# One decoder block on one core: 24 instead of 16 expert blocks loaded whole, and their schedule

## The reference, cut to what matters

```python
eid = take_along_axis(cand_i, pos)           # (token, head, 16)
gate = softmax(top_s)
act = gelu(einsum('bthkd,btd->bthk', peer_u[eid], h))
out = einsum('bthk,bthkd->btd', gate * act, peer_v[eid])
x = x + out
```

## Time and profile before

| what | value |
|---|---|
| runs shown | 2595.43, 2602.96, 2604.31 us, median 2602.96 |
| profiled execution, its own time | 2600.41 us |
| its span | 2598.8 us |
| PE, DVE, ACT, POOL busy in the span | 78%, 64%, 35%, 34% |
| moved by DMA | 746.40 MB, mean 287 GB/s |
| packets of the gathers' queue (q0) | 75584, 483.52 MB |

### The profile page before, as it was taken

How to read it: one execution, slowest core, us unless ns; L and a number is a source line. 1 busy time by engine, 2 the same in 40 slices (tenths; PEclk the granted TensorE clock), 3 DMA queues, 4 the chain that set the end, 5 groups by cost and what they waited for, 6 DMA issues and landing times.

```text
span 2598.8 us, 33274 instructions
## 1 busy us (share of the span) xinstructions
PE 2033.2 (78%) x11327; PEld 1511.2 (58%) x11327; DVE 1667.3 (64%) x2540; ACT 915.1 (35%) x1828; POOL 878.8 (34%) x631
## 2 busy tenths in 40 slices
PE   7999999999999999999975455365465278666568
PEld 6899888988988988978962122132232046422222
DVE  5888647766666766775687666666755488644440
ACT  4565555555554554545433133213331110111100
POOL 1400011001001001040044755555665676555662
PEclk9999999999999999999987677677777666688889
DMA  5454566565565566566689999999999999999997
GB/s 182 124 162 129 174 186 190 171 201 182 166 202 186 166 197 187 168 204 206 230 334 392 404 414 387 410 402 392 412 413 404 386 413 409 397 393 409 410 413 278
DMA packets 216630, 746.40 MB, mean 287 GB/s; under 512 B 27600, under 2 KB 62792, under 8 KB 152648
## 3 DMA queue, kind: packets, MB, share of 16 engines
q0 software_dynamic: 75584, 483.52, 46.3%
q1 hardware_dynamic: 140448, 261.36, 31.4%
q10 hardware_dynamic: 496, 0.23, 0.0%
HBM read 806.74 MB, written 4.26 MB: 312 GB/s over the span
## 4 chain that ended last, share of the span: by engine, by line
PE 50%; DMA 29%; POOL 7%; DVE 7%; issue 6%; ACT 1%; POOLq 0%; DVEq 0%; ACTq 0%
DMA u_slots<-in_peer_u_dram,eid 18%; DMA v_slots<-in_peer_v_dram,v_eid 10%; PE accA L1905 4%; PE accA L1907 4%; PE accA L1906 4%; PE accB L1905 4%; PE accB L1907 4%; PE accB L1906 4%; POOL v_slots L807 3%; POOL u_slots L783 3%; DVE dot_junk L1689 2%; PE accB L1899 2%; PE accB L1898 2%; PE accB L1897 2%; PE small L1915 2%
## 5 line engine op out<-in xcount | busy, mean ns | idle before, releaser
L1689 DVE CUSTOM_DVE_ANT_0 dot_junk<-u_slots,h 128x2048 bf16<-128x2048 f32 x240 | 550.0, 2292 | 429.1 <-DMA u_slots<-in_peer_u_dram,eid 416.8
L1256 DVE TENSOR_TENSOR w_lo<-w_raw,w_hi 128x1024 fp32r<-128x1024 f32 (+1 forms) x409 | 508.2, 1252 | 283.8 <-ACT w_hi L859 282.3
L859 ACT ACTIVATE w_hi<-w_raw 128x1024 fp32r<-128x1024 f32 (+1 forms) x420 | 442.2, 1057 | 408.6 <-PE accB L1907 121.5
L783 POOL DMA_INDIRECT u_slots<-in_peer_u_dram,eid x256 | 332.6, 1299 | 461.0 <-DVE dots L1689 302.9
L807 POOL DMA_INDIRECT v_slots<-in_peer_v_dram,v_eid x252 | 413.9, 1643 | 123.6 <-issue 88.8
L2358 PE MATMUL accA<-v_slots,weight 128*32 128x512 f32 x512 | 114.1, 1040 | 319.6 <-DMA v_slots<-in_peer_v_dram,v_eid 301.5
L2358 PE MATMUL small<-v_slots,weight 128*32 128x512 f32 x496 | 115.0, 999 | 198.8 <-DMA v_slots<-in_peer_v_dram,v_eid 198.8
L2358 PEld LDWEIGHTS accA<-v_slots,weight 128*32 128x32 f32 x512 | 21.7, 157 | 378.8 <-issue 378.8
L1185 ACT ACTIVATE gelu_s<-dots 32x4 f32<-32x4 f32 x256 | 52.9, 207 | 463.7 <-DVE dots L1689 460.9
L2358 PEld LDWEIGHTS small<-v_slots,weight 128*32 128x32 f32 x496 | 22.1, 153 | 255.3 <-issue 255.3
L752 POOL TENSOR_TENSOR y_skip<-x_tok,per_head_g 128x512 f32<-128x512 f32 x16 | 24.2, 1529 | 424.1 <-ACT x_tok L1087 424.1
(11 more groups left out here) (420 smaller groups left out, 4568.9 us busy)
## 6 DMA issues: line engine op xcount, KB each, us to landing
w_raw<-in_w_in_dram SPq DMA_DIRECT2D x168, 512.0 KB, 3.6
w_raw<-in_w_in_dram SPq DMA_DIRECT2D x128, 256.0 KB, 3.0
w_raw<-in_w_o_ssm_dram SPq DMA_DIRECT2D x64, 512.0 KB, 4.2
w_raw<-in_w_o_attn_dram SPq DMA_DIRECT2D x32, 512.0 KB, 5.0
w_raw<-in_w_out_dram SPq DMA_DIRECT2D x32, 512.0 KB, 4.7
w_raw<-in_w_peer_q_dram SPq DMA_DIRECT2D x32, 512.0 KB, 5.0
dense_raw<-in_peer_u_dram SPq DMA_DIRECT2D x16, 1024.0 KB
dense_raw<-in_peer_v_dram SPq DMA_DIRECT2D x16, 1024.0 KB
```

The source lines that it names most:

```text
L783: pool.indirect_dma_start(u_slots[:, n % U_RING, :], None, peer_u[0], bass.IndirectOffsetOnAxis(ap=eid[:, u, k:k + 1], axis=0), bounds_che ...
L859: act.activation(w_hi[:, slot, :, 0:w], w_raw[:, slot, :, 0:w], ACT.Copy).then_inc(hi_split, 1)
L1256: dve.tensor_tensor(w_lo[:, slot, :, 0:w], w_raw[:, slot, :, 0:w], w_hi[:, slot, :, 0:w].bitcast(F32), ALU.subtract).then_inc(lo_split, 1)
L1689: dve.tensor_tensor_reduce(dot_junk[:, :] if i >= PK else slot, slot, h2[:, u // PH, :], 1.0, 0.0, ALU.mult, ALU.add, dots[:, u % 2, k:k + ...
```

## The change

The last 24 blocks are loaded whole, no longer 16. `FIRST_DENSE` follows, so rows of 8 more blocks are skipped by the gathers. U blocks are worked at periods 4 to 27, one each; `turn_picks` at 27; gates at 28 to 35; V blocks at 36 to 54, one a period and two in every fourth. Chunks of tokens are 16 instead of 32, two chunks a period; the first 8 chunks' gates go to `small` and `pair_d`, the last 8 to A and B, and PE starts unit 8 only when the first 8 are weighed. Three of four one-hots are made by ACT (Square with the negated id as bias, then Relu of one minus it), the fourth by DVE. Ids from unit 2 on are spread by DVE. In ACT's loop `unit_gelu(u + 1)` now stands behind the whole-block work of all four periods, `copy_picks` behind it. `merge_first` is at dot 149, `merge_dense` at dot 244 and no longer behind the last weights.

```diff
-DENSE = 16
+DENSE = 24
+DENSE_HEAD = 16
-HOT_RING = 6
-CHUNK = 32
+HOT_RING = 4
+CHUNK = 16
+    dense_head = sb("dense_head", [P, DENSE_HEAD, T])
+    dense_tail = sb("dense_tail", [P, DENSE - DENSE_HEAD, T])
-        PICKS_AT, CHUNKS_AT, DENSE_V_AT = 33, 36, 45
-        MERGE_DOT, HOT_DOT, GATED_LAG = 151, 164, 7
+        U_AT, PICKS_AT, CHUNKS_AT, DENSE_V_AT = 4, 27, 28, 36
+        MERGE_DOT, GATE_DOT, WEIGH_DOT, LAST_MERGE_DOT = 149, 131, 135, 244
+        CHUNKS_EACH = 2
         def dense_u(period):
-            return period // 2 if period < 2 * DENSE and period % 2 else None
+            return period - U_AT if 0 <= period - U_AT < DENSE else None
+        def dense_v(period):
+            n = period - DENSE_V_AT
+            first = n + (n + 1) // 4
+            return range(min(first, DENSE), min(first + (2 if n % 4 == 2 else 1), DENSE)) if n >= 0 else range(0)
+        def gate_bank(c):
+            return ((small, pair_d) if c < CHUNKS // 2 else (A, B))[c % 4 // 2][:, c % 2, :]
...
                 for v in top_units(u):
                     unit_softmax(v)
-                    spread_ids(v)
...
+            def hot_of(j):
+                if j == 0:
+                    act.wait_ge(iota_ready, 1)
+                    act.wait_ge(picks_back, 2)
+                if j >= HOT_RING:
+                    act.wait_ge(hot_used, j - HOT_RING + 1)
+                for i in range(HOT):
+                    t, token = (HOT * j + i) // P, (HOT * j + i) % P
+                    ins = act.activation(hot[:, j % HOT_RING, i, :], iota_k[:, :], ACT.Square,
+                                         bias=pick_t[:, 2 + t, token:token + 1])
+                ins.then_inc(hot_squared, 1)
+                act.wait_ge(hot_squared, j - j // HOT_RING + 1)
+                act.activation(hot[:, j % HOT_RING, :, :], hot[:, j % HOT_RING, :, :], ACT.Relu, scale=-1.0,
+                               bias=iota_k[:, 1:2]).then_inc(hot_ready, 1)
+            def hots(period):
+                first = (period - CHUNKS_AT) * CHUNKS_EACH * HOTS
+                if 0 <= first < CHUNKS * HOTS:
+                    for j in range(first, first + HOT_RING - 1):
+                        hot_of(j)
...
             for u in range(UNITS):
-                for q in (0, 1):
+                for q in range(4):
                     dense_blocks(4 * u + q)
-                selected(u + 1)
-                if 4 * u + 1 == PICKS_AT:
-                    copy_picks()
+                    hots(4 * u + q)
+                    if q == 1:
+                        selected(u + 1)
                 if u + 1 < UNITS:
                     unit_gelu(u + 1)
-                for q in (2, 3):
-                    dense_blocks(4 * u + q)
+                if 4 * u + 3 == PICKS_AT:
+                    copy_picks()
...
                 dve.scalar_tensor_tensor(eid[:, all_units, :], part[:, 0, 0:n, :], float(NK), part[:, 1, 0:n, :],
                                          ALU.mult, ALU.add).then_inc(unit_ids, n)
+                if n > 1:
+                    dve.wait_ge(unit_ids, units[-1] + 1)
+                    for u in units:
+                        for lanes, ids in spread(u):
+                            ins = dve.tensor_copy(lanes, ids)
+                        ins.then_inc(v_ids, 1)
...
             def after_dot(i):
+                n = i - GATE_DOT
+                if n >= 0 and n % 2 == 0 and n // 2 < CHUNKS:
+                    if n == 0:
+                        dve.wait_ge(iota_ready, 2)
+                    gates_of(n // 2)
+                n = i - GATE_DOT - 2
+                if n >= 0 and n % 4 == 0 and n // 4 < CHUNKS // CHUNKS_EACH:
+                    last_hot_of(n + HOT_RING - 1)
+                n = i - WEIGH_DOT
+                if n >= 0 and n % 2 == 0 and n // 2 < CHUNKS:
+                    weigh_dense(n // 2)
                 if i == MERGE_DOT:
                     merge_first()
...
+                if i == LAST_MERGE_DOT:
+                    merge_dense()
...
             weights_of(UNITS - 1)
-            merge_dense()
             merge_last()
...
             for u in range(UNITS):
                 t, h = u // PH, u % PH
                 pe.wait_ge(weighed, u + 1)
+                if u == PH:
+                    pe.wait_ge(a_ready, 2 * (CHUNKS // 2))
```

More of the change, by code:

```diff
@@ L441, in hybrid_block @@
         hot_ready = sem("hot_ready")
+        hot_squared = sem("hot_squared")
+        hot_made = sem("hot_made")
         hot_used = sem("hot_used")
@@ L489, in top_units, with last_top @@
             return range(2 * u, 2 * u + 2) if u < 8 else range(0)
+        def last_top(u):
+            return top_units(u) and top_units(u)[-1] == UNITS - 1
         V_IN_U = PK * (UNITS - 1)
@@ L1133, in spread_ids @@
                 act.wait_ge(unit_ids, u + 1)
[L1134 to L1137, removed]
+                for lanes, ids in spread(u):
+                    ins = act.activation(lanes, ids, ACT.Copy)
                 ins.then_inc(v_ids, 1)
@@ L1742, in picks_of @@
                 steps.mark(dve.tensor_scalar(pick_hlf[:, 0, :], pick_hl[:, 0, :], -float(NK - DENSE), None, ALU.add))
-                step(dve.tensor_copy(pick_hlf[:, 1, :], pick_hl[:, 1, :]))
+                step(dve.tensor_scalar(pick_hlf[:, 1, :], pick_hl[:, 1, :], -1.0, None, ALU.mult))
                 dve.sem_inc(picks_ready, 1)
@@ L1778, in after_dot, with weigh_dense @@
-            def after_dot(i):
+                                  iota_n[:, :].unsqueeze(1).broadcast_to([P, HOT, NK]),
+                                  ALU.is_equal).then_inc(hot_made, 1)
+            def weigh_dense(c):
+                if c == 0:
+                    dve.wait_ge(d_taken, DENSE)
+                dve.wait_ge(hot_used, HOTS * (c + 1))
+                tokens = slice(CHUNK * c, CHUNK * (c + 1))
+                gates = gate_bank(c)[:, 0:CHUNK * DENSE].rearrange("p (t b) -> p b t", b=DENSE)
+                for a, b in ((dense_head, slice(0, DENSE_HEAD)), (dense_tail, slice(DENSE_HEAD, DENSE))):
+                    dve.tensor_tensor(a[:, :, tokens], a[:, :, tokens], gates[:, b, :], ALU.mult).then_inc(a_ready, 1)
@@ L1859, in _ @@
                     weights_of(u - 1)
-                    if top_units(u - 1):
+                    if top_units(u - 1) and not last_top(u - 1):
                         scale_gates(top_units(u - 1))
-                        if u == PH:
-                            picks_of()
                 dotted = [4]
@@ L2309, in dense_gates @@
                         ins = pe.matmul(o[:, n * DENSE:(n + 1) * DENSE], hot[:, j % HOT_RING, i, :],
-                                        hot_gate[:, k % 2, n, :], start=True, stop=True)
+                                        hot_gate[:, c % 2, n, :], start=True, stop=True)
                     ins.then_inc(hot_used, 1)
@@ L2334, in beside @@
                     dense_dots(dense_u(period))
-                if period == 4 * PH - 1:
-                    pe.wait_ge(d_taken, DENSE)
                 if period == PICKS_AT:
                     turn_picks()
[L2339 to L2342, removed]
+                for c in range(CHUNKS_EACH * (period - CHUNKS_AT), CHUNKS_EACH * (period - CHUNKS_AT + 1)):
+                    if 0 <= c < CHUNKS:
+                        dense_gates(c)
+                for i in dense_v(period):
+                    dense_sums(i)
             pe.wait_ge(small_free_act, sf_act_l + 4 + 4 * NT)
```

83 lines of the change are left out of this document (45 added, 38 removed).

## The result

The changed kernel takes **2637.42 us** (median of 4, 2633.88 to 2639.89) against 2603.62 (2595.43 to 2604.31) for the kernel before beside it: ratio 1.0143, 95% interval 1.0127 to 1.0158. It is 1.4% slower; 2625 was forecast. The profiled execution has a span of 2637.2 against 2598.8, +38.4.

A forecast was written before the change was run, and what follows sets the result against it. DMA was taken to bound the second half, so a period lasts as long as its bytes. Terms -41.5 - 10 + 60 + 8 + 5 + 1 = +22.5 on 2600.41 gave 2622.9, plus 2.55 for the median: 2625 us, range 2572 to 2662.

The forecast's parts named there:

- Bytes: Gathers and loads: 33.6 MB fewer gathered, 16.8 MB more loaded, at 404 GB/s -41.5 us (40 to 43).
- The end: Last gathers: V blocks end at period 54, so POOL no longer waits for PE there; -10 us (-6 to -12).
- The gelu: Ends of periods 7, 11, 15, 19, 23, 27: gelu behind the fourth U block stalls DVE; 6 x 10 = +60 us (18 to 90).
- Periods without blocks: Periods 28 to 35 and 55 to 63: POOL may not keep up with the bytes; 0.5 us each, +8 (0 to +20).
- The start: Periods 0 to 3, where DVE bounds: 32 copies of ids come to DVE; +5 us (0 to +10).
- (a): Gathers in flight cover the gelu stalls, 3 us lost each: 2583 us, faster by 0.8%; chance 0.25.
- (b): The gelu stalls are shorter, say 6 us each: 2601 us, no change; chance 0.22.
- (c): POOL bounds whenever DVE has caught up, 4.6 us per pair of issues: +69.5, 2672 us; chance 0.13.
- (d): The added whole blocks are picked less than evenly: worth 1 or 2 us only; no chance of its own given.

The follow-up runs named there:

- e1: Changed kernel with ACT's `unit_gelu(u + 1)` moved ahead of the whole-block work of period 4u + 3: 2573.57 us, ratio 0.9898 to the kernel before.
- e4: e1 with the spreading of ids given back to ACT, ahead of the gelu: 2589.98 us, ratio 0.9956 to the kernel before.
- e9: e1 with the ids given back to ACT, behind the gelu and ahead of the fourth U block: 2578.97 us, ratio 0.9912 to the kernel before.
- e8: e1 with gathers fetching only the lower half of the table, output wrong: 2401.11 us, ratio 0.9231 to the kernel before.
- e5: Changed kernel with DVE doing eight dots instead of four ahead of the weights in units 2 to 7: 2591.93 us, ratio 0.9969 to the kernel before.

## Why the prediction came out right, step by step

The direction and the mechanism held: a late gelu, DVE's dots behind it, POOL's issue behind them, DMA dry. That the number came near is in part luck, as the largest term has two errors that cancel. The sum gave +22.5, the span grew by 38.4. By the terms:

**Bytes, -41.5: -44 measured.** Right in size, again through two errors that cancel. The eight blocks hold 14% more picks than an even share (4664 rows for 4096), so 38.2 MB go and not 33.6. At 327 ns less 9 a row they would have saved 92 us of engine time, and saved 79.7, as the rows that are still fetched take 3 ns longer each. The loads add 35.8 (816.0 to 851.8 by the rows of q1). That skipped rows move nothing holds to 4 bytes a row. The rate in the last full stretch fits: 401 GB/s against 408.

**The end, -10: -8.** DMA was idle 18.5 us in the last 109 us of before (share 0.83 from 2490 on) and 10.2 in the 85 of after. One price in this term was misread: four matmuls in 1.98 us are 7.9 a block, not 7.

**The gelu, +60: +71.** This is the step that decides. Its path came as it was put. From V 11 the trace of after has the first transpose at +6.2 (6.3 in the sum), ACT's last step done at +16.0 (16.1), the gelu at +22.9 (23.1), the dot done at +29.8 (29.9) and the issue at +30.7 (30.2). V 12 starts 23.9 us behind V 11, where 25 was said. But the sum has six stalls of 10 us, and the trace has **five of 13 to 15**. The dry time, put at 8 plus 2 for what the bytes don't say, was too small: it is 13.2 in this place, as the bytes in flight last some 20 us instead of 23.5 (the share is 0.49 from +19 to +21.5) and flow again at about +33 instead of +31.5. And the count was one too high: at period 27 DVE waited 14.9 us for the picks, with 3.4 us dry. What I held, that idle time of a bound engine is never given back, fits: by the single packets DMA is idle for 71.3 us less in `e1` than in after, and the span is 67.6 shorter.

**Periods without blocks, +8: +6, but for another reason.** All of it lies in the gates' stretch (7.6 idle, against 1.8 in `e1` and none in the earlier trace rows): it follows the sixth place, not POOL, which the term was put down to. Of POOL as the limit of these periods nothing shows. Periods 55 on go at 16.5 and 15.7 us (V 2552.6, 2569.1, 2584.8) with DMA full.

**The start, +5: +5.** 7.0 idle against 1.8; in `e1` it is the same 7.8, so neither the gelu nor its stalls make it. DVE is busy 80% there. In `e4` and `e9`, where ACT spreads the ids, it is 4.4 (share 0.95), so about 3 of the 5 are the copies, which take 0.19 us each and not 0.17.

**Not in the sum: +5.** What the stretch of the U blocks has idle beside the five stalls, 76 less 71; 3 of it stand just ahead of the sixth place.

Measured terms: -44 - 8 + 71 + 6 + 5 + 5 = +35, near the 38.4; the last 3 I can't place. The sum fell 16 short of the span and the forecast 12 of the median, mainly by the gelu's term, 11.

**The rivals.** (a), stalls covered at 3 each, is refuted: 12. Its argument, the merge stall that lost 2.3, was right for its length: the five gelu waits of up to 9.6 us in `e4` cost some 2 each. (b), shorter stalls, is refuted by the same number. (c), POOL as the bound at 4.6 us a pair, is refuted by `e8`: 3.95. Its parts add up to 4.9, not 4.6, and what was wrong in it is that each V issue was made to begin when a dot ends; in the trace of `e8` two or three issues in a row fall between dots at 0.99 us each. That an issue and a dot exclude each other does show: in the trace of before the 138 issues that begin while a dot runs end, nearly all, 0.87 us behind its end and have a mean of 2.65 us, the 374 others 1.03. It does not show for the copies of ids: 15 issues of after that begin in one take 0.99. The Trainium skill, "SBUF — State Buffer", section "Who interferes with whom", puts the lock on the whole instruction down to VectorE's two-port modes. Beside it stands a contention of a VectorE instruction with two SBUF inputs, as the dot is, with a GpSimd instruction that reads SBUF. The trace of after fits the second better: six issues that begin in a one-hot of 1.22 us, a plain `tensor_tensor` with two inputs, take 1.86 in the mean. In either case the step from that rule to the sum of (c) did not follow, as `e8` has both the long issues and 3.95 us a pair. (d), unevenly picked blocks: more picks than even, not fewer.

## What to carry to other kernels

Where one engine works in a fixed order, a step appended to the end of a period is paid by whoever reads what stands behind it. Follow that chain, ACT's gelu to DVE's weights to DVE's dots to the slot to POOL's issue, to the engine that feeds the bound, and compare its stall with what is in flight. Here POOL held for 8 to 10.5 us left DMA dry for 0 to 5 us, 12.4 and 12.7 for 7 and 3 (`e5`, after), 19.9 for 11 (`e4`), and 22 for 13 to 15. The cure was to move one call a period earlier in ACT's order, which turned +1.4% into -1.0%. An idle wait that is under what is in flight is hardly worth removing: three experiments that did so gained nothing that could be told. And count the stalls in the trace before dividing by them: five of 14 and six of 10 give nearly the same sum.

## What the runs showed of the hardware that I had not expected

A row that an indirect gather skips by its bound stays as a packet of 4 bytes that takes 9 ns, where a fetched row of 8 KB takes 324; the count of packets is unchanged. But leaving rows out made the fetched ones take longer in the mean, 372 ns in `e8` for 328 in `e1`. Halving the gathers' table took 175.3 MB and 337 us of engine time away, and only 172 us of time, as POOL's issues were next. And an issue of POOL that begins while a dot of 2.29 us runs ends 0.87 us behind it and takes 2.65 in the mean, where one that begins outside takes 1.03 in the mean.
